# Expert retrieval of a decoder layer: retrieval spread over more slots, groups of the second table's rows placed at other slots, and two spare row homes given from the second table to the first

## The reference, cut to what matters

```python
def peer_ffn(h, w_q, keys1, keys2, u_tab, v_tab):
    ...
    s1 = jnp.einsum('bshq,hnq->bshn', q[..., 0, :], keys1)
    s2 = jnp.einsum('bshq,hnq->bshn', q[..., 1, :], keys2)
    v1, i1 = lax.top_k(s1, PEER_TOPK)
    v2, i2 = lax.top_k(s2, PEER_TOPK)
    ...
    best, pos = lax.top_k(cand, PEER_TOPK)
    expert_idx = jnp.take_along_axis(cand_idx, pos, axis=-1)
    gates = jax.nn.softmax(best, axis=-1)
    ...
        u = jnp.take(u_tab, ix, axis=0)
        act = jax.nn.gelu(jnp.einsum('chkd,cd->chk', u, hx), approximate=False)
        vv = jnp.take(v_tab, ix, axis=0)
        return jnp.einsum('chk,chkd->cd', gx * act, vv)
```

## Time and profile before

| | us |
|---|---|
| median of 3 runs | 1755.1 (1751.66 to 1757.19) |
| the profiled execution, own time | 1757.74 |
| its span (first to last instruction) | 1756.0 |
| PE busy | 1476.3 (84%) |
| DVE busy | 1204.6 (69%) |
| POOL busy | 703.4 (40%) |
| ACT busy | 543.5 (31%) |
| gathers, share of 16 DMA engines over the span | 62.4% |
| plain loads, the same | 29.1% |

### The profile page before, as it was taken

How to read it: one execution, slowest core, us unless ns; L and a number is a source line. 1 busy time by engine, 2 the same in 40 slices (tenths; PEclk the granted TensorE clock), 3 DMA queues, 4 the chain that set the end, 5 groups by cost and what they waited for, 6 DMA issues and landing times.

```text
span 1756.0 us, 20157 instructions
## 1 busy us (share of the span) xinstructions
PE 1476.3 (84%) x7320; PEld 977.8 (56%) x7320; DVE 1204.6 (69%) x2134; ACT 543.5 (31%) x1589; POOL 703.4 (40%) x626
## 2 busy tenths in 40 slices
PE   2979999989999998898899757756699898988865
PEld 1648987878788875666676434424343333333321
DVE  5877886889889988898454477768644545454462
ACT  3003432764311256343210146436411010110132
POOL 1001011000122344555666567556643555454461
PEclk9979999999999999999999966767799999999888
DMA  9999997849969679999999999998999999999996
GB/s 337 386 386 406 403 376 305 308 175 369 356 225 359 233 302 372 379 372 391 358 406 375 357 372 394 343 377 325 376 356 392 359 402 395 352 415 412 406 353 257
DMA packets 149806, 624.46 MB, mean 356 GB/s; under 512 B 33994, under 2 KB 38272, under 8 KB 86528
## 3 DMA queue, kind: packets, MB, share of 16 engines
q0 software_dynamic: 82976, 427.52, 62.4%
q1 hardware_dynamic: 66732, 195.67, 29.1%
HBM read 797.54 MB, written 2.10 MB: 455 GB/s over the span
## 4 chain that ended last, share of the span: by engine, by line
PE 39%; DMA 23%; DVE 22%; issue 6%; POOL 6%; ACT 3%; DVEq 1%; SPq 1%; POOLq 0%; ACTq 0%
DMA u_rows<-in_peer_u,expert 12%; DVE u_rows L2030 10%; PE ps L1216 8%; PE ps L1164 7%; DMA v_rows<-in_peer_v,expert_rows 7%; PE ps L457 5%; PE ps L1066 5%; PE ps L909 4%; POOL v_rows L800 4%; DVE first_acc L486 3%; PE ps L903 2%; PE ps L1131 2%; DMA ada_first<-in_w_ada 2%; DMA dense_rows<-in_dense_v 1%; DVEq L1950 1%
## 5 line engine op out<-in xcount | busy, mean ns | idle before, releaser
L2030 DVE SCALAR_TENSOR_TENSOR u_rows<-u_rows,h 128x1024 f32<-128x1024 f32 (+1 forms) x416 | 593.5, 1467 | 379.9 <-DMA u_rows<-in_peer_u,expert 365.4
L800 POOL DMA_INDIRECT u_rows<-in_peer_u,expert x256 | 333.8, 1304 | 348.0 <-DVE u_rows L2030 265.8
L800 POOL DMA_INDIRECT v_rows<-in_peer_v,expert_rows x210 | 278.5, 1326 | 193.5 <-PE ps L1164 140.1
L1164 PE MATMUL ps<-v_rows,diag 128*32 128x512 f32 x1680 | 266.8, 704 | 84.9 <-DMA v_rows<-in_peer_v,expert_rows 75.8
L1216 PE MATMUL ps<-dense_rows,dense_weight 128*128 128x512 f32 x640 | 286.5, 605 | 13.7 <-DVE dense_sums L2109 6.6
L457 PE MATMUL ps<-h2T,dense_rows 128*128 128x256 f32 x1280 | 284.2, 383 | 3.8 <-ACT dense_weight L1562 3.8
L457 PEld LDWEIGHTS ps<-h2T,dense_rows 128*128 128x128 f32 x1280 | 243.5, 191 | 52.3 <-issue 16.1
L1216 PEld LDWEIGHTS ps<-dense_rows,dense_weight 128*128 128x128 f32 x640 | 121.7, 193 | 178.1 <-issue 169.0
L1164 PEld LDWEIGHTS ps<-v_rows,diag 128*32 128x32 f32 x1680 | 68.1, 126 | 229.8 <-issue 229.4
L308 POOL DMA_DIRECT2D ada_late<-in_w_ada x61 | 32.3, 530 | 304.4 <-DVE ada_acc L322 262.5
L322 DVE SCALAR_TENSOR_TENSOR ada_acc<-ada_late,cact,ada_acc 128x2048 f32<-128x2048 f32 x57 | 133.8, 2348 | 17.1 <-DMA ada_late<-in_w_ada 15.9
(11 more groups left out here) (308 smaller groups left out, 1842.8 us busy)
## 6 DMA issues: line engine op xcount, KB each, us to landing
ada_late<-in_w_ada POOLq DMA_DIRECT2D x61, 1024.0 KB, 7.8
dense_rows<-in_dense_u SPq DMA_DIRECT2D x40, 1024.0 KB, 18.3
dense_rows<-in_dense_v SPq DMA_DIRECT2D x40, 1024.0 KB
ada_first<-in_w_ada SPq DMA_DIRECT2D x64, 512.0 KB, 11.7
ring<-in_w_in SPq DMA_DIRECT2D x10, 2048.0 KB, 24.7
ring<-in_w_o SPq DMA_DIRECT2D x8, 2048.0 KB, 15.0
ring<-in_w_peer_q SPq DMA_DIRECT2D x8, 2048.0 KB, 14.7
opened<-in_w_in SPq DMA_DIRECT2D x8, 1024.0 KB, 13.0
```

Source lines behind the costliest of these rows:

```text
L800: nc.gpsimd.indirect_dma_start(buf[:, :], None, table, bass.IndirectOffsetOnAxis(ap=places, axis=0), bounds_check=last_sparse, oob_is_err= ...
L1164: ins = nc.tensor.matmul(ps[rows, k, :], diag[n % len(diag)][:, :], v_slot(n)[0][:, 512 * k:512 * k + 512], start=first, stop=last)
L2030: ins = nc.vector.scalar_tensor_tensor(out=u_rows[b][:, lo:hi], in0=u_rows[b][:, lo:hi], scalar=1.0, in1=h2[:, q // H, lo:hi], op0=ALU.mul ...
```

## The change

It moves work between slots and homes between the tables. No instruction on data is added or removed.

- **Retrieval.** Job 1 is spread over slots 0 to 11, job 2 over 12 to 26, and each later job over 5 or 6 slots (16/3 on average) up to slot 95. The exponents of the jobs 2 to 5 move on ACT from the time of the queries into the slot loop.
- **Groups.** group_order starts at 39, goes in steps of 68/13 = 5.2 slots up to group 12 (key 101), and from group 13 (key 107) in steps of 61/24 = 2.5 slots up to key 168. Behind 168 it is as before.
- **Tiles.** tile_key goes from 31 to 103.
- **v homes.** SPARE now holds two homes (dense_rows[0:2]), for slots 52 to 115. The gather distances (AHEAD and the constant behind row_before) are smaller.
- **u homes.** The two spare_rows go to u: one for slots 104 to 139, one for 104 to 255. gather_u waits for the dot of the slot that was in its home, and the first use of a spare home for S39.
- **Waits.** spread_weights(q), which writes the buffer that the diagonals of job q - 2 read, now waits for them. The copies of g2b on ACT, which write over a spare home, wait for the last dot in it and no longer for a group.

```diff
-    LEAD, LAG = 31, 20
+    LEAD, LAG = 39, 20
     HOT_KEY, HOT_END = 107, 168
-    LEAD_GROUPS, LAG_GROUPS = (HOT_KEY - LEAD) // QUADS, (HOT_END - LAG) // QUADS
+    LEAD_GROUPS, LAG_GROUPS = 13, (HOT_END - LAG) // QUADS
...
-    SPARE = [(76, 124), (76, 124), (76, 116), (76, TAIL)]
+    SPARE = [(52, 116), (52, 116)]
+    U_SPARE = [(104, 140), (104, SLOTS)]
     G2_KEY = 146
-    AHEAD = 5, 9, 6
+    AHEAD = 5, 6, 4
 
     def group_order(g):
-        between = HOT_KEY + (g - LEAD_GROUPS) * (HOT_END - HOT_KEY) // (LAG_GROUPS - LEAD_GROUPS)
-        return max(QUADS * g + LAG, min(QUADS * g + LEAD, between))
+        if g < LEAD_GROUPS:
+            return LEAD + g * (HOT_KEY - LEAD) // LEAD_GROUPS
+        return max(QUADS * g + LAG, HOT_KEY + (g - LEAD_GROUPS) * (HOT_END - HOT_KEY) // (LAG_GROUPS - LEAD_GROUPS))
 
     def gather_key(n):
 
         if n < 2:
-            return 24
+            return 27
         if n < len(v_rows):
-            return 31
+            return 33
...
-        return max(key, group_order(row_before[n] // QUADS) + 4) if row_before[n] is not None else key
+        return max(key, group_order(row_before[n] // QUADS) + 2) if row_before[n] is not None else key
...
     def tile_key(i):
-        return 22 + 2 * i
+        return 31 + 37 * i // 20
...
     def retrieval_slots(q):
 
-        return (5 * q - 5, 5) if q < H else (5 * H - 5 + 4 * (q - H), 4)
+        first = (0, 0, 12, *(27 + 16 * k // 3 for k in range(QJOBS - 2)))
+        return first[q], first[q + 1] - first[q]
...
+    u_places = list(zip(u_rows + spare_rows[2:], u_landed + spare_landed[2:]))
+    u_slots = [[] for _ in u_places]
+    u_home, u_before = [], []
+    for n in range(SLOTS):
+        open_now = list(range(len(u_rows))) + [len(u_rows) + k for k, (first, end) in enumerate(U_SPARE) if first <= n < end]
+        b = min(open_now, key=lambda b: u_slots[b][-1] if u_slots[b] else -1)
+        u_home.append((b, len(u_slots[b])))
+        u_before.append(u_slots[b][-1] if u_slots[b] else None)
+        u_slots[b].append(n)
...
             def gather_u(n):
-                b = n % len(u_rows)
+                b, use = u_home[n]
+                buf, landed = u_places[b]
...
-                if n >= len(u_rows):
-                    pool.wait_ge(dots, n - len(u_rows) + 1)
-                gather(expert[:, n // TOPK, n % TOPK:n % TOPK + 1], u_rows[b], u_landed[b], peer_u[0])
+                if u_before[n] is not None:
+                    pool.wait_ge(dots, u_before[n] + 1)
+                elif b >= len(u_rows):
+                    full(pool, f"S{DENSE - 1}")
+                gather(expert[:, n // TOPK, n % TOPK:n % TOPK + 1], buf, landed, peer_u[0])
...
-                if u == 6:
-                    for q in range(2, 5):
-                        exponent(q)
-                if u == 7:
-                    exponent(5)
 
             def spread_weights(q):
                 act.wait_ge(weighted, q + 1)
+                if q >= 2:
+                    act.wait_ge(diagonal, TOPK * (q - 1))
...
-                    if n == sum(retrieval_slots(q)) and q >= 6:
+                    if n == sum(retrieval_slots(q)) and q > 1:
                         exponent(q)
...
                 if n == G2_KEY + 1:
-                    group_used(act, last_before_tail(len(v_rows) + 2) // QUADS)
+                    act.wait_ge(dots, u_slots[len(u_rows)][-1] + 1)
```

More of the change, by code:

```diff
@@ L611, in retrieval_slots @@
     def retrieval_slots(q):
-        return (5 * q - 5, 5) if q < H else (5 * H - 5 + 4 * (q - H), 4)
+        first = (0, 0, 12, *(27 + 16 * k // 3 for k in range(QJOBS - 2)))
+        return first[q], first[q + 1] - first[q]
     def due(key, count, n):
         return (i for i in range(count) if key(i) == n)
-    row_places = list(zip(v_rows + spare_rows, v_landed + spare_landed))
+    row_places = list(zip(v_rows + spare_rows[:2], v_landed + spare_landed[:2]))
     row_slots = [[] for _ in row_places]
@@ L636, in v_slot @@
             b = n - LAST
-            return u_rows[b], u_landed[b], 16 * (SLOTS // len(u_rows) + 1)
+            return u_rows[b], u_landed[b], 16 * (len(u_slots[b]) + 1)
         if TAIL <= n < TAIL + 4:
@@ L824, in gather_v @@
                 if n >= LAST:
-                    pool.wait_ge(dots, n + 1)
+                    pool.wait_ge(dots, u_slots[n - LAST][-1] + 1)
                 elif TAIL <= n < TAIL + 6:
@@ L2017, in dot @@
             def dot(n):
-                b, use = n % len(u_rows), n // len(u_rows)
+                b, use = u_home[n]
+                rows, landed = u_places[b]
                 q, k = divmod(n, TOPK)
-                dve.wait_ge(u_landed[b], 16 * (use + 1))
+                dve.wait_ge(landed, 16 * (use + 1))
                 if n == 0:
@@ L2029, in dot @@
                 for lo, hi, total in parts:
-                    ins = nc.vector.scalar_tensor_tensor(out=u_rows[b][:, lo:hi], in0=u_rows[b][:, lo:hi], scalar=1.0,
+                    ins = nc.vector.scalar_tensor_tensor(out=rows[:, lo:hi], in0=rows[:, lo:hi], scalar=1.0,
                                                          in1=h2[:, q // H, lo:hi], op0=ALU.mult,
```

## The result

The changed kernel takes 1837.8 us (median of 4 runs, 1833.39 to 1842.85); the kernel before, run beside it, 1754.8. The ratio is 1.0475, with a 95% interval of 1.0439 to 1.0511: 83 us slower, where 10 had been forecast. The profiled execution has a span of 1839.1 us.

The account below looks back on a forecast made before the run. The prediction took DMA bytes as the bound, so only idle DMA time could be won. Rows owed (43 us) less the earlier last tile (35) gave +8, taken as +10 with the ramp: 1755 + 10 = 1765 us, range 1738 to 1792.

Parts of the forecast that it names:

- Part 1: Early slots: thin retrieval starts slot 32 near 619 us instead of 650; PE waits 5 us for ACT instead of 3.8.
- Part 2: PE up to the last tile (S39): 328 us of work plus 30 of waits, ending at 960 us instead of 995.2.
- Part 4: POOL waits about 20 us for the last tile, mostly hidden; the hole at 980 grows 0 to 10; ramp +5.
- Part 5: Last tile to key 168: 16 groups take 197 us, 8 periods of 15 take 120; gathers end behind; +10 us taken.
- third rival: Close stretch: POOL stands at v gathers until DVE passes the group's key; 1795 us; chance 0.15 together with rival 4.
- rival 4: Early gathers land too late, ACT holds PE 25 us at the third tile; S39 at 980, 1785 us; 0.15 with third rival.
- Part 6: Behind key 168: 5 u and 6 v homes instead of 4 and 7, gain and loss cancel; 0 us.
- Rivals 1: Faster: the hole at 580 is filled and nothing lost for it; S39 ends at 942, 1740 us; chance 0.29.
- 2: A wash: S39 ends near 950, the early gain is what the 24 rows owe; 1755 us; chance 0.20.
- part 3: At the last tile 24 fewer v gathers are issued; moving them costs 43 us against 35 won, net +8.

Follow-up runs that it names:

- the run with 2 alone: Kernel before with thin retrieval and the change's u homes, the constant behind row_before at 2 instead of 4: 1813.6 us, ratio 1.0342.
- the run with 27: Kernel before with thin retrieval alone, LEAD 27 instead of 31 (groups 4 slots earlier), first v gathers and spare homes moved too: 1739.6 us, ratio 0.9919.
- 1740: Kernel before with thin retrieval and the two spare homes given to u; groups, tiles and gather keys as before: 1740.3 us, ratio 0.9926.
- 1788: Changed kernel with the constant behind row_before at 4 instead of 2: 1787.8 us, ratio 1.0218.

## Why the prediction was wrong

The sign was right and the size wrong by 73 us, outside the range. By the steps:

- **Part 1, retrieval: right in kind, late by 12 us.** Slot 32 began at 631.5, not 619. Spreading the jobs filled the hole and costs nothing later; alone it is worth 14 us. Dot 31 ended near 628, not 620. ACT made it worse in a way I had named and priced at 5 us: at its n = 32 the exponent of the next job, the gelu and the table loads come ahead of tile_out(0). ACT waited 12.0 us for DVE before that exponent, until 628.5, and PE stood 12.7 us at the third tile. "One wait replaces the other" was wrong by 9 us.
- **Part 2, PE up to the last tile: 981 us, not 960.** The first tile began at 604, not 601. The work was 340 us, not 328: the 40 tiles took 292.4 us, 7.3 each, with a granted clock of 0.96 on average from 601 to 981, and the 13 groups took 47.3. The waits were 39 instead of 27: 15 for ACT, not 5, 24 for dense rows, not 12, and none for v rows, not 10. The upper bound for dense rows had been 30 and was the better guess: the stretch was less full, but PE waited for them all the same. The runs show where the gain went. Thin retrieval and the u homes bring the end of the last tile from 995 to 976, fewer groups ahead of it to 949; the tile keys of the change take it back to 973, and the distances to 981.
- **Part 4, POOL's stand: 25.3 us**, about 20 expected. It was said to be hidden but for 0 to 10; the DMA share was 0.39 from 960 to 980, so 12 were lost in these 20 us alone.
- **Part 5 is the step that failed.** For groups 13 to 28 I took the bytes, 12.3 us a period, because eight homes let a group's rows wait for the group two before. It was 14.1 (999.6 to 1224.7 us, 16 groups). These 16 periods took 28 us more than forecast, and 23 of them went away with the constant at 4 (12.7 a period): POOL's standing, which I had put at nothing here, was the larger part. From group 29 to 36 the period was 15.1, as forecast; only the last, to group 37, which has a dense piece of the second table in it, took 25.7, where it had taken 19.3 before. From the last tile to group 37 it took 374 us, not 332. The chain after shows the link that I had read from the earlier trace rows, now with one issue of POOL more before the gather that lands last, which is what the forecast of 15 was made of:

```profile
1238.39 5.39 PE ps L1180 x32
1244.05 0.99 POOL v_rows L813
1245.04 0.30 issue
1245.34 7.88 DMA v_rows<-in_peer_v,expert_rows
1253.47 6.38 PE ps L1180 x32
1260.11 1.17 POOL v_rows L813
```

  So the chain with six homes was right, and what was missing is the standing with eight. That POOL would stand until DVE had passed the group's key was there only as the third rival, with 30 us and, together with the fourth, a chance of 0.15. POOL stood for groups for 110 us between 985 and 1340 us, in 20 waits. The condition that I gave, a wait above the 11 us that the queue covers, was wrong: one of the 20 was above it, 12.3 us, and the time was lost all the same. The windows and the run with 2 alone agree with the rival; its price of 30 us was too low against the 50 and 73 that the constant measured.
- **Part 6: 0 was wrong.** From group 37 to the end it took 483 us, where the kernel before took 464 and the forecast with its rows owed had 474. The share was 0.94 instead of 0.98. I had let the homes cancel (one more for u, one less for v) and had looked at the number of homes, not at the constant, which acts there as well. With 4 in its place the share is 0.98 again.
- **The hardly mentioned edit.** In the prediction the constant, 4 to 2, is one clause of a rival. It was the largest term. Reading "the gather distances are smaller", I took them for small; the kernel before had a sign of it, 140 us of POOL's wait at v gathers, which the prediction passes over.

Of the 73 us that the profiled execution took beyond the forecast, 21 lie before the last tile ends, 42 from there to group 37, and 9 behind it.

Rivals 1, 2 and 4: none held as a whole. The last tile came 14 us earlier than before, not 53 or 45. It ended at 981, which is close to the 980 of rival 4, but early dots did come sooner, ACT held PE for 12.7 us at the third tile and not for 25, and 1785 us missed the rest. The Trainium skill, "DMA: Bandwidth & Descriptors", Specifications, has about 358 GB/s as the HBM limit of a core; the windows of 389 GB/s over 170 us and 394 over 360 us disagree, as those of before did.

**Open.** The 25 us that the groups' placement costs with the tile keys of before were not split into rows owed and close stretch, nor was it told apart from the first v keys and the slots of the spare homes, which moved with it. What is shown is that it lies behind the last tile: with this placement that tile ends 27 us earlier, and the kernel 25 us later. That is 52 us lost behind it, where part 3 of the prediction had 43 us for the rows owed. That its cost is not in proportion to rows owed is suggested by the run with 27, which gained nothing. Nor was it shown whether PE is late in the close stretch by v rows or by DVE's one-hot matrices; both waits are in the traces.

## What to carry to other kernels

Where one engine issues two streams of gathers in order, the place of a waiting gather in that order is a price for both streams. Too close behind the event it waits for, the engine stands and starves the other stream; too far, its own rows come late. Measure that distance step by step: from 2 to 3 and from 3 to 4 a slot was worth 45 and 29 us here, and from 4 to 6 it cost 11. The worth of buffers depends on that distance. The two homes, held by the waiting stream (v) instead of the one held up (u), were worth 37 us at 2, and at 4 nothing on one placement and 7 us on the other; at 5 they were worth 14. When a change moves many constants, price each by asking who stands behind the wait, before pricing the bytes, and take apart what is bundled: the first part alone was a gain of 14 us, and with one step of the constant the other way a kernel of 1729 us.

## What the runs showed of the hardware

Nothing unexpected in the prices. A group took 3.6 us of PE at the higher granted clock and mostly 4.6 to 6.6 where the windows grant 0.70 to 0.73 on average; a tile took 7.0. The DMA engines gave 408 to 417 GB/s in windows of 20 us in which they were full, in the kernels before and after and in the runs of 1740 and 1788. Unexpected was that a less busy DMA did not bring a dense tile's load in time: with the share at 0.90 instead of 0.97, PE waited for one nine times, 23.8 us in all and 3.9 at the longest. The kernel before, with two tiles between groups, had no such wait in this stretch.
